# Seven modulation units move from the norms between dense stages into the two mixers' stretches, and four halvings of weights move behind the norms

## The reference

```python
# block 1
mod = silu(c) @ w_ada + b_ada                      # 6 x 1024 modulations
h = rms_norm(x, g_pre_mix) * (1 + sc_m) + sh_m
y = hybrid_mixer(h, ...)                           # attention, compression, indexer
x = x + ga_m * rms_norm(y, g_post_mix)
h = rms_norm(x, g_pre_ffn) * (1 + sc_f) + sh_f     # "nf" in the kernel
x = x + ga_f * rms_norm(swiglu(h, w_gate_up, w_down), g_post_ffn)
# block 2
mod = silu(c_2) @ w_ada_2 + b_ada_2 ; mod_c = silu(c_ctx) @ w_ada_2 + b_ada_2
hc = rmsnorm(ctx, norm1_w) * (1 + mod_c[1]) + mod_c[0]      # "nc"
h = rmsnorm(x, norm1_w) * (1 + mod[1]) + mod[0]             # "n2"
x = x + mod[2] * token_mixer(h, states_of(hc), ...)         # gated linear attention, retention
h2 = rmsnorm(x, norm2_w) * (1 + mod[4]) + mod[3]            # "nr"
x = x + mod[5] * expert_choice_ffn(h2, 16 experts)
out = rmsnorm(x, final_norm_w)
```

## Time and profile before

| | us |
|---|---|
| median of 3 runs | 1548.68 |
| lowest and highest | 1544.26, 1552.39 |
| the profiled execution: its time | 1549.95 |
| the profiled execution: its span | 1548.2 |
| PE busy in it | 1102.5 |
| DVE, ACT, POOL busy in it | 469.3, 295.8, 48.9 |

### The profile page before, as it was taken

The page is one execution under the profiler, slowest core; times in us unless marked ns, Lnnn a source line. Parts: engine busy times, 40 slices in busy tenths (PEclk is TensorE's granted clock), DMA queues, the critical chain, the costliest instruction groups (busy, mean ns, idle before and its releaser), DMA issues.

```text
span 1548.2 us, 14239 instructions
## 1 busy us (share of the span) xinstructions
PE 1102.5 (71%) x6030; PEld 621.9 (40%) x6030; DVE 469.3 (30%) x931; ACT 295.8 (19%) x494; POOL 48.9 (3%) x60
## 2 busy tenths in 40 slices
PE   4788977699889897897785576556555556655564
PEld 2576755477566684685544431101111111111121
DVE  1546664353341563445675410000000000000002
ACT  2422432342331333242303110000000000000000
POOL 0010000100000000002301000000000000000000
PEclk9897987789999997898796786886888786678897
DMA  9753255554334345455220669999999999999994
GB/s 387 281 215 137 82 191 204 197 178 163 111 110 168 138 177 190 161 182 195 82 82 0 271 277 426 426 428 427 425 427 427 427 426 426 426 426 429 423 429 201
DMA packets 41440, 417.26 MB, mean 270 GB/s; under 512 B 4960, under 2 KB 4960, under 8 KB 8224
## 3 DMA queue, kind: packets, MB, share of 16 engines
q1 hardware_dynamic: 38160, 405.75, 65.3%
q10 hardware_dynamic: 3216, 10.60, 1.8%
HBM read 415.28 MB, written 1.05 MB: 269 GB/s over the span
## 4 chain that ended last, share of the span: by engine, by line
PE 46%; DMA 37%; DVE 11%; ACT 4%; issue 2%; POOL 1%; ACTq 0%; POOLq 0%; DVEq 0%
DMA ring<-in_w_egu 24%; DMA ring<-in_w_ed 12%; PE PS L597 8%; PE PS L598 8%; PE PS L599 8%; PE PS L1177 4%; PE PS L550 3%; PE PS L879 3%; PE PS L537 3%; DVE arena L1223 2%; DVE ringR L1301 1%; PE PS L1208 1%; DMA CT<-in_consts 1%; ACT ringR L2093 1%; PE PS L716 1%
## 5 line engine op out<-in xcount | busy, mean ns | idle before, releaser
L1177 PE MATMUL PS<-ring,arena 128*32 128x512 f32 (+1 forms) x1536 | 231.4, 738 | 158.8 <-DMA ring<-in_w_egu 157.8
L597 PE MATMUL PS<-ringR,arenaR 128*128 128x512 f32 (+1 forms) x520 | 215.6, 415 | 31.5 <-DVE arenaR L1289 30.6
L598 PE MATMUL PS<-ringR,arenaR 128*128 128x512 f32 (+1 forms) x520 | 209.6, 403 | 0.0
L599 PE MATMUL PS<-ringR,arenaR 128*128 128x512 f32 (+1 forms) x520 | 208.5, 401 | 0.0
L1301 DVE TENSOR_TENSOR ringR<-ring,ringR 128x2048 fp32r<-128x2048 f32 (+1 forms) x66 | 148.4, 2255 | 155.8 <-ACT ringR L2093 155.8
L1177 PEld LDWEIGHTS PS<-ring,arena 128*32 128x32 f32 x1536 | 49.0, 128 | 331.8 <-DMA ring<-in_w_egu 252.4
L1208 PE MATMUL PS<-ring,arena 128*32 128x512 f32 x704 | 115.7, 791 | 81.7 <-DMA ring<-in_w_ed 80.3
L1223 DVE SCALAR_TENSOR_TENSOR arena<-arena,PS 128x256 f32<-128x256 f32 (+2 forms) x68 | 33.5, 498 | 420.7 <-ACT arena L2490 400.4
L2093 ACT ACTIVATE ringR<-ring 128x2048 fp32r<-128x2048 f32 (+1 forms) x66 | 123.3, 1882 | 120.2 <-PE PS L599 119.0
L597 PEld LDWEIGHTS PS<-ringR,arenaR 128*128 128x128 f32 x520 | 100.8, 194 | 59.8 <-DVE arenaR L1289 31.8
L537 PE MATMUL PS<-CT,arena 128*128 128x128 f32 (+1 forms) x352 | 64.6, 333 | 64.8 <-DVE arena L1223 33.6
(11 more groups left out here) (319 smaller groups left out, 953.4 us busy)
## 6 DMA issues: line engine op xcount, KB each, us to landing
ring<-in_w_egu SPq DMA_DIRECT2D x64, 2048.0 KB, 26.2
ring<-in_w_ed SPq DMA_DIRECT2D x44, 2048.0 KB, 25.8
ring<-in_w_ada SPq DMA_DIRECT2D x48, 1024.0 KB, 4.9
ring<-in_w_egu SPq DMA_DIRECT2D x32, 1536.0 KB, 21.2
ring<-in_w_in SPq DMA_DIRECT2D x22, 1024.0 KB, 4.9
ring<-in_w_gu SPq DMA_DIRECT2D x22, 1024.0 KB, 4.8
ring<-in_w_dn SPq DMA_DIRECT2D x10, 1024.0 KB, 4.8
ring<-in_w_out SPq DMA_DIRECT2D x8, 1024.0 KB, 4.9
```

The lines of the kernel that those rows point to most:

```text
L597: mm(o, xh(k, t), hi[:, c], start=k == 0, stop=False)
L598: mm(o, xh(k, t), s.viewr[:, c], start=False, stop=False)
L599: i = mm(o, xl(k, t), hi[:, c], start=False, stop=k == nk - 1)
L1177: i = mm(PS[32 * ee:32 * ee + 32, b + a_, 0:fw], XEv[:, k, 32 * E:32 * E + 32], wv[:, ee, a_, :], start=k == 0, stop=k == 7, tile_position ...
```

## The change

The counts of steps in `ATT` and `GLA` rise (units 28 to 31 go into `ATT`, units 34 to 36 into `GLA`), `NF` is a plain norm, and `N2` runs two whole units ahead of the norm. The order of the weights in the ring follows: units 28 to 31 come ahead of `out1`, units 34 to 36 behind `in2`. On DVE `low` of the first `gu` slot comes behind the norm, and that of the second behind the halves; so too for `in2`. On ACT `top_half` of the second slot moves behind the norm. Two affine vectors (`nc`, `n2`) are made later. POOL's `rstd` has one addition in place of a multiplication and an addition, and ACT's squares are scaled. One wait of DVE for its own last result is added in `head_norm`.

```diff
-    n = {"p": 3, "f": 40, "0": 18, "1": 18, "i": 24, "d": 7, "c": 14}
+    n = {"p": 3, "f": 48, "0": 18, "1": 18, "i": 24, "d": 7, "c": 14}
...
-    n = {"u": 8, "n": 5}
-    nf = list("un") + ["u"] * 7 + ["n"] * 4
...
-    n2 = list("un") + ["u"] * 9 + ["n"] * 4
-    n = {"f": 22, "g": 17, "r": 17}
+    n2 = list("uuuunnnnn")
+    n = {"f": 28, "g": 17, "r": 17}
...
         for i in range(len(PLAN["out1"])):
             want_dense("out1", i)
-        for j in range(4):
-            want_ada(n_ada + j)
-        n_ada += 4
...
-        for j in range(5):
+        for j in range(2):
             want_ada(n_ada + j)
-        n_ada += 5
+        n_ada += 2
         for i in range(len(PLAN["in2"])):
             want_dense("in2", i)
-        for j in range(11):
+        for j in range(14):
             want_ada(n_ada + j)
...
# vector
-            low("gu", 0)
-            low("gu", 1)
             w.wait_ge(*loaded("gqf"))
             tt(mods[:, 1024:2048], mods[:, 1024:2048], gq, ALU.mult).then_inc(*sig("v out1 gq", 1))
-            lanes = {"u": adas(28, 32), "n": norm("nf", Xv, Y1, st2, (4, 5, 6, 0), affs[:, 16:32], hT)}
-            for k in NF:
-                next(lanes[k])
-            affine("nc", mc2, 0, 1, PR("n1"), affs2[:, 32:48])
-            affine("n2", mc2, 0, 0, PR("n1"), affs2[:, 0:16])
+            for _ in norm("nf", Xv, Y1, st2, (4, 5, 6, 0), affs[:, 16:32], hT):
+                pass
             for j in range(4):
                 if j % 2 == 0:
                     w.wait_ge(*at("a nf h", 2 * j))
+                if j == 0:
+                    low("gu", 0)
                 halves("gu", j, rnd(HH3)[:, 512 * j:512 * j + 512], pieces(hT, 512 * j))
+
+            low("gu", 1)
+            affine("nc", mc2, 0, 1, PR("n1"), affs2[:, 32:48])
+            affine("n2", mc2, 0, 0, PR("n1"), affs2[:, 0:16])
...
-            low("in2", 0)
-            low("in2", 1)
-            lanes = {"u": adas(32, 37), "n": norm("n2", Xv, junk3, st3, (4, 5, 6), affs2[:, 0:16], hT2)}
+            lanes = {"u": adas(32, 34), "n": norm("n2", Xv, junk3, st3, (4, 5, 6), affs2[:, 0:16], hT2)}
             for k in N2:
                 next(lanes[k])
+            low("in2", 0)
...
                 tt(rnd(hT2)[:, c], hT2[:, c], rnd(HH4)[:, c], ALU.subtract).then_inc(*sig("v in2 xl", j))
+            low("in2", 1)
             cp(GZx[0:32, :], PS[0:32, 6, 0:256]).then_inc(*sig("v in2 z"))
...
                 w.wait_ge(*at("g ret gate", n))
+                chain()
...
# scalar
             top_half("gu", 0)
+            for _ in norm("nf", Xv, Y1, st2, (4, 5, 6, 0), affs[:, 16:32], hT, [at("v out1 x", 0), at("v out1 x", 1)]):
+                pass
             top_half("gu", 1)
...
             top_half("in2", 0)
-            top_half("in2", 1)
...
             for k in N2:
                 next(lanes[k])
+            top_half("in2", 1)
...
# gpsimd
-            def rstd(S, *index, dst, ms, d):
-                e.tensor_scalar(dst, ms, 1.0 / d, EPS, ALU.mult, ALU.add).then_inc(*sig(f"g {S}"))
+            def rstd(S, *index, dst, ms):
+
+                e.tensor_scalar(dst, ms, EPS, None, ALU.add).then_inc(*sig(f"g {S}"))
```

More of the change, by code:

```diff
@@ L79, in schedules @@
     gla += "f" * (n["f"] - done["f"])
-    return att, nf, ffn, n2, gla
-ATT, NF, FFN, N2, GLA = schedules()
+    return att, ffn, n2, gla
+ATT, FFN, N2, GLA = schedules()
 LATE = ("Mf", "Mb", "mskf", "mskb", "Rp", "Rm", "cosR", "sinR", "H4")
@@ L813, in compress @@
                     yield
-            lanes = {"p": prepare(), "f": adas(8, 28), "0": attention(0), "1": attention(1), "i": indexer(), "d": prepare_d(), "c": compress()}
+            lanes = {"p": prepare(), "f": adas(8, 32), "0": attention(0), "1": attention(1), "i": indexer(), "d": prepare_d(), "c": compress()}
             for k in ATT:
@@ L832, in tensor @@
                 pass
-            lanes = {"u": adas(28, 32), "n": norm("nf", Y1, (4, 5, 6, 0), lambda k: [])}
-            for k in NF:
-                next(lanes[k])
+            for _ in norm("nf", Y1, (4, 5, 6, 0), lambda k: []):
+                pass
             def gated_T(g):
@@ L949, in tensor @@
                 pass
-            lanes = {"u": adas(32, 37), "n": norm("n2", junk3, (4, 5, 6), lambda k: [at("a gu gt", 10), at("a ctx sr", 3), at("v ctx sr", 2)] if k < 6 else [at("a n2 h", 0)])}
+            lanes = {"u": adas(32, 34), "n": norm("n2", junk3, (4, 5, 6), lambda k: [at("a gu gt", 10), at("a ctx sr", 3), at("v ctx sr", 2)] if k < 6 else [at("a n2 h", 0)])}
             for k in N2:
@@ L1107, in retention @@
                 yield
-            lanes = {"f": adas(37, 48), "g": gla(), "r": retention()}
+            lanes = {"f": adas(34, 48), "g": gla(), "r": retention()}
             for k in GLA:
@@ L2068, in norm @@
                 for t in range(2):
-                    act(two(junk)[:, t, :], src[:, t, :], ACT.Square, accum_out=st[:, t:t + 1]).then_inc(*sig(f"a {S} sq", t))
+                    act(two(junk)[:, t, :], src[:, t, :], ACT.Square, scale=1.0 / 32, accum_out=st[:, t:t + 1]).then_inc(*sig(f"a {S} sq", t))
                 w.wait_ge(*at(f"g {S} rs"))
@@ L2154, in prepare @@
                 for t in range(2):
-                    i = act(QT[:, 128 * t:128 * t + 128], prv[:, t, 1816:1944], ACT.Square, accum_out=stp[:, t:t + 1])
+                    i = act(QT[:, 128 * t:128 * t + 128], prv[:, t, 1816:1944], ACT.Square, scale=128 ** -0.5, accum_out=stp[:, t:t + 1])
                 i.then_inc(*sig("a p sq"))
@@ L2260, in scalar @@
             top_half("gu", 0)
+            for _ in norm("nf", Xv, Y1, st2, (4, 5, 6, 0), affs[:, 16:32], hT, [at("v out1 x", 0), at("v out1 x", 1)]):
+                pass
             top_half("gu", 1)
-            lanes = {"u": adas(28, 32), "n": norm("nf", Xv, Y1, st2, (4, 5, 6, 0), affs[:, 16:32], hT, [at("v out1 x", 0), at("v out1 x", 1)])}
-            for k in NF:
-                next(lanes[k])
             def ffn():
@@ L2360, in scalar @@
             top_half("in2", 0)
-            top_half("in2", 1)
-            lanes = {"u": adas(32, 37), "n": norm("n2", Xv, junk3, st3, (4, 5, 6), affs2[:, 0:16], hT2, [at("v dn x", 0), at("v dn x", 1)])}
+            lanes = {"u": adas(32, 34), "n": norm("n2", Xv, junk3, st3, (4, 5, 6), affs2[:, 0:16], hT2, [at("v dn x", 0), at("v dn x", 1)])}
             for k in N2:
                 next(lanes[k])
+            top_half("in2", 1)
             w.wait_ge(*at("pe n2 tr", 6))
@@ L2499, in scalar @@
                 w.wait_ge(*at("v fin x", t))
-                act(two(junkf)[:, t, :], Xv[:, t, :], ACT.Square, accum_out=st4[:, t:t + 1]).then_inc(*sig("a fin sq", t))
+                act(two(junkf)[:, t, :], Xv[:, t, :], ACT.Square, scale=1.0 / 32, accum_out=st4[:, t:t + 1]).then_inc(*sig("a fin sq", t))
         def gpsimd(e):
@@ L2515, in gpsimd @@
             w.wait_ge(*at("a nx sq", 1))
-            rstd("nx", dst=st1[:, 2:4], ms=st1[:, 0:2], d=1024)
+            rstd("nx", dst=st1[:, 2:4], ms=st1[:, 0:2])
             w.wait_ge(*at("pe in1 slot", len(PLAN["in1"]) - 1))
@@ L2519, in gpsimd @@
             w.wait_ge(*at("a p sq"))
[L2520 removed]
+            rstd("p", dst=stp[:, 2:4], ms=stp[:, 0:2])
             for t in range(2):
                 w.wait_ge(*at("a out1 sq", t))
[L2523 removed]
+                rstd("out1", t, dst=s21[:, 2 + t:3 + t], ms=s21[:, t:t + 1])
             w.wait_ge(*at("a nf sq", 1))
[L2525 removed]
+            rstd("nf", dst=st2[:, 2:4], ms=st2[:, 0:2])
             w.wait_ge(*at("a nc sq", 1))
[L2527 removed]
+            rstd("nc", dst=stc[:, 2:4], ms=stc[:, 0:2])
             for t in range(2):
                 w.wait_ge(*at("a dn sq", t))
[L2530 removed]
+                rstd("dn", t, dst=s22[:, 2 + t:3 + t], ms=s22[:, t:t + 1])
             w.wait_ge(*at("a n2 sq", 1))
[L2532 removed]
+            rstd("n2", dst=st3[:, 2:4], ms=st3[:, 0:2])
             w.wait_ge(*at("pe in2 z"))
```

12 lines of the change are left out of this document (5 added, 7 removed).

## The result

The changed kernel takes 1561.7 us (median of 6 runs, 1556.6 to 1566.9) against 1550.7 of the kernel before in the same runs; the ratio is 1.0076, with a 95% interval of [1.0045, 1.0106], which is +11.8 us on 1550. The forecast was 1551.7, +3.0, with a range of 1542 to 1561. The sign is that of the forecast sum, but the size is four times as large, and outside the 0.5% (7.7 us) that the forecast called no change. The forecast stood on a median of 1548.7 for the kernel before, which is 1550.7 here: 2.0 of the 10.0 us between 1551.7 and 1561.7 are that difference, and no effect of the change. The rival *the lower clock stays* had said 1559.

A forecast was written before the change was run, and what follows sets the result against it. The prediction took the kernel as a chain of delays before 863 us and DMA-bound from 901.6 us; 15.9 - 12.3 + 0.5 - 11.8 + 1.0 + 9.6 + 0.1 = +3.0 us gave 1551.7, range 1542 to 1561.

The forecast's parts named there:

- the lower clock stays: Rival: PE's clock stays low before the tail of `GLA`, which costs 14.4, and through z; +10.4, 1559; chance 0.2.
- What bounds the kernel: Before 863 us a chain, so any delay there moves the end equally; from 901.6 us DMA is 97% busy.
- Where the units go: No moved unit lands under a mixer: four run in a row at the end of `ATT`, three at that of `GLA`.
- The first tail, +15.9: End of `ATT`: four more units in a row at 3.97 us each, at the lower clock, cost 15.9 us.
- The norm before `gu`, -12.3: Without units and with POOL's pair sooner, transposes start 14.0 us earlier; the low half's place gives back 1.6; -12.3 used.
- The context, +0.5: Behind `gu`'s start, the later affine vectors for `nc` delay PE's transposes of the context: +0.5 us, bounds 0 and 1.5.
- The norm before `in2`, -11.8 + 1.0: With two units ahead of the norm, transposes start 11.8 us sooner; product z may meet the lower clock, +1.0.
- The second tail, +9.6: End of `GLA`: three more units at the full clock cost 8.4, plus 1.2 if the last fall back; bounds 8.4 and 14.4.
- three signs of being wrong: A pitch of 2.7 in the first tail, `gu` waiting for its low half, or units ending up under the mixers.
- The first tail was not at the full clock: Rival for the end of `ATT`: at the full clock four units cost 10.8, sum -2.1, 1546.6; chance 0.15.
- The units do not vanish in the mixers: Rival, here denied: waits absorb the extra steps and both tails cost nothing, -22.5, 1526; chance 0.05.
- No transfer came late: Rival, here denied: `out1` or `in2` weights come late behind the units, +5, 1557; chance 0.05.

The follow-up runs named there:

- e1: Kernel before with only units 28 to 31 moved to the end of attention, so the norm before `gu` runs without units: 1.0032, +5.0 us.
- e3: Kernel before with only DVE's order of low halves and affine vectors as in the change, all units staying: 0.9996, -0.6 us.
- e2: Kernel before with only two units put ahead of the norm before `in2` and three more in the second tail: 1.0035, +5.4 us.
- e4: Kernel before with both moves of units and nothing else of the change: 1.0073, +11.3 us.
- g2: Changed kernel with a second turn for units in each round of the attention weave alone: 1.0019, +2.9 us.
- f1: Changed kernel with filler products on PE behind both steps of the last nine attention units and last five second-mixer units: 0.9998, -0.3 us.
- h1: e2 with filler products on PE before the two head norms and behind both steps of the second tail's five units: 0.9965, -5.4 us.
- g1: Changed kernel with two turns for units in each round of both weaves: 1.0081, +12.5 us.
- g3: Kernel before, with nothing of the change but two turns for units in each round of both weaves: 1.0168, +26 us.

## Why the prediction was wrong

**What bounds the kernel** was right. Every us lost before `out2` is still there when the experts begin: from the start of `out2` to that point it is 63.3 us and was 63.1.

**Where the units go** was right, and it is the heart of the matter: the four and three units stand in a row at the ends of the stretches, and nothing hides them.

**The first tail, +15.9,** measured +17.4 in the profile and +16.4 in e1. In the changed kernel's profile the clock fell one unit sooner, which is 1.0 of the difference, and in both it is 0.6 us longer from the last unit to `out1`, where ACT begins its high halves later. The transfers of `out1` were covered, as costed.

**The norm before `gu`, -12.3,** measured -12.0 (-13.7 to the transposes and +1.7 behind them). POOL's pair came down from 3.72 to 1.04. The reading of its cause was half right. DVE's two `low` end at 297.28 and lay over the first instruction of the pair only. Over the second lay DVE's product of the gains, an instruction with two inputs in SBUF as well.

```profile
297.19 1.22 DVE L1633 TENSOR_TENSOR arena<-arena 128x1024 f32<-128x1024 f32 x1
```

In the changed kernel this product ends at 317.80 and the low halves come later, so neither lies over POOL's pair, which begins at 319.03.

**The context, +0.5,** measured +2.0. e1 shows 0.8 without any reordering on DVE, e3 shows 1.2 with nothing else. I had the second at 0.5, and none of the first; why the feed-forward takes 0.8 longer behind the moved units was not tried.

**The norm before `in2`, -11.8 + 1.0,** measured -11.7 to the transposes, and z +1.9. The clock did not stay low through z, it rose within it.

**The second tail, +9.6: this is the step that failed.** It measured +14.5, and 4.9 of the 8.7 us by which the sum was short are there. The forecast priced its three units more at the full clock (8.4) and added 1.2 in case the last ones fall back. It took the full clock from the earlier trace rows, where the clock comes back during the first of the two units of that tail, and from the sentence that what stands before this unit is unchanged. It is not. Unit 45, whose second step stood there, is a row unit; now it is unit 42, a column unit, and so is the first one of the row, 43. The step directly before, in the kernel before and then in the changed one:

```profile
824.40 1.06 PE L556 MATMUL PS<-PT,CT 128*128 128x256 f32 x2
```
```profile
827.33 0.85 PE L554 MATMUL PS<-CT,PT 128*128 128x2 f32 x4
```

In the three profiles with the old order and without filler (before, e1, e3) the clock comes back within the first unit of the tail. In the five with the new one and without filler ahead of the tail (changed, e2, e4, g2, f1) that unit takes 1.94, and two to five units run at 1.2 GHz. Three against five without an exception speak for something in the order and not for luck, but nothing was run to single out the kind of the unit. It was the rival *the lower clock stays*, at its upper price of 14.4, that came true; I gave it 0.2. Why the clock stays low there stays open. That it is the clock, and not a late transfer or a late add, is shown by h1, where only PE's idleness was taken away.

**The rest of the 8.7 us** is the first tail (1.5), the context (1.5), `out1` (0.6), the norm before `gu` (0.3), and 1.1 in the norm before `in2`, which `in2` itself gave back. None of the three signs of being wrong that the forecast named came: the pitch in the first tail was 3.98, `gu`'s last wait was for the halves of the activations (L1283) and not for its low half, and no unit was under a mixer. It had named none for the second tail's pitch.

**The other rivals.** The first tail was not at the full clock. The units do not vanish in the mixers: they did not in the change, and when put there they cost 1.6 to 2.3 us each in attention (g2, g1) and more than in a row in the second mixer (g1, g3). No transfer came late.

The Trainium skill (TensorE: Matmul & The Clock Gate, What's actually happening) says that the throttled state is the default, and that activity releases it. The trace agrees in f1's first tail and h1's second, where PE makes products while it would wait and every unit takes 1.07 us. For work with waits between, this case has both: with waits of about 0.5 us, three units of the first tail before take 1.07 and two 1.94. Had I costed the second tail like the first, at the lower clock throughout, it would have had 14.4, and the sum +7.8: still 4 short of the +11.8.

## What to carry to other kernels

A lane that is no main lane of a weave (one that the weave does not wait for) gets no more turns than the others need; count the turns before moving work into it, since the surplus lands at the end as a row of bare round trips. When a chain of small steps over several engines moves, price it at the lower clock of TensorE, at 4 us a unit here and not 2.7, unless PE has other products to make in its waits. And when units change places, look at which kind of unit now stands where, not only at how many. Filling TensorE's waits with products that nobody reads was worth more here (8 to 12 us) than any placing of the units.

## What was not expected of the hardware

The kernel before gives 1544.2 to 1545.5, 1547.5 to 1550.2 or 1552.6 to 1554.9 us in 35 runs, three groups with gaps between them, and from end to end nearly as much as the change is worth. (In 39 further runs the groups are there again, with one run between two of them, at 1551.4.) That the moment when the clock changes level makes these groups is argued, not shown, since there is one profile of this kernel. In the profiles the products of units 2 to 7, ahead of everything that differs, take 1.07 or 1.94 us each, and `in1` starts up to 7 us apart.

TensorE stayed at the lower level without being idle for long: in the changed kernel's second tail it was busy for 1.98 and 2.04 of 3 us in the two stretches shown, its longest wait between the units was 0.61 us, and it stayed at 1.2 GHz through all five units, 19 us. In the first tail it did so through seven, 27 us.
